# A Mixture-of-Experts stage: gate columns in one buffer, up columns in the other, and narrow down products in four column groups

## What is computed

```
def moe_swiglu(t, router, w_gate, w_up, w_down):
    logits = (t @ router).astype(jnp.float32)
    top_logits, top_idx = lax.top_k(logits, TOP_K)
    gates = jax.nn.softmax(top_logits, axis=-1)
    combine = jnp.sum(jax.nn.one_hot(top_idx, N_EXPERTS, dtype=jnp.float32) * gates[..., None], axis=1)
    out = jnp.zeros_like(t)
    for e in range(N_EXPERTS):
        out = out + combine[:, e:e + 1].astype(t.dtype) * swiglu(t, w_gate[e], w_up[e], w_down[e])
    return out
```

## Time and profile before

| | |
|---|---|
| three runs | 3126.87, 3130.53, 3133.26 us (median 3130.53) |
| span of the profiled execution | 3127.4 us |
| TensorE busy | 3027.5 us, 97% of the span |
| TensorE weight loads | 2197.5 us, 70% |
| VectorE, ScalarE busy | 1227.9 us, 482.9 us |
| read from HBM | 632.70 MB |
| chain that ended last | TensorE 84%, SyncE's queue 4%, VectorE 4%, DMA 3% |

### The profile page before, as it was taken

One profiled execution on the slowest core, in us unless ns is written; L12 is line 12 of the kernel. 1 busy time (PEld: TensorE's weight loads), 2 busy tenths in 40 slices (PEclk: granted clock), 3 DMA queues, 4 the chain that ended last, 5 costly groups with the idle time before them and its releaser, 6 DMA issues.

```text
span 3127.4 us, 44307 instructions
## 1 busy us (share of the span) xinstructions
PE 3027.5 (97%) x18487; PEld 2197.5 (70%) x18487; DVE 1227.9 (39%) x2576; ACT 482.9 (15%) x1092; POOL 109.9 (4%) x122
## 2 busy tenths in 40 slices
PE   7999998999999999999999999998999999999998
PEld 3566666588697677696786795876767677677765
DVE  2566666457466433366466365232001101101001
ACT  2332332010010023200212100221000000000001
POOL 1111112000000000000000000000000000000000
PEclk8999999999999999999999999998999999999999
DMA  7333116465355522364310465426999999999996
GB/s 252 119 109 128 54 55 260 158 221 164 125 187 166 160 68 74 94 203 162 103 58 14 123 202 162 126 64 214 379 381 377 355 382 375 341 380 380 337 379 253
DMA packets 418569, 636.83 MB, mean 204 GB/s; under 512 B 11950, under 2 KB 305429, under 8 KB 411069
## 3 DMA queue, kind: packets, MB, share of 16 engines
q1 hardware_dynamic: 413021, 612.49, 56.8%
q0 software_dynamic: 5344, 21.46, 2.0%
HBM read 632.70 MB, written 1.20 MB: 203 GB/s over the span
## 4 chain that ended last, share of the span: by engine, by line
PE 84%; SPq 4%; DVE 4%; DMA 3%; issue 1%; ACT 1%; DVEq 1%; PEld 1%; PEldq 0%; ACTq 0%
PE PS L1085 11%; PE PS L4106 11%; PE PS L1644 7%; PE PS L1105 7%; PE PS L4127 5%; PE PS L4113 5%; PE PS L1038 4%; PE PS L4153 3%; SPq L882 2%; PE PS L708 2%; PE PS L2220 2%; PE PS L3592 2%; PE PS L1119 2%; PE PS L2216 2%; PE PS L1794 1%
## 5 line engine op out<-in xcount | busy, mean ns | idle before, releaser
L1013 DVE TENSOR_TENSOR scratch<-scratch,PS 128x128 f32<-128x128 f32 x112 | 32.2, 288 | 618.2 <-ACT scratch L1003 618.2
L1644 PE MATMUL PS<-XT,WH 128*128 128x512 f32 x512 | 241.6, 597 | 1.7 <-ACT XT L485 1.7
L4106 PEld LDWEIGHTS PS<-scratch,WO 128*128 128x128 f32 x1792 | 208.6, 192 | 24.9 <-issue 24.3
L4106 PEld LDWEIGHTS PS<-scratch,WF 128*128 128x128 f32 x1792 | 202.2, 192 | 23.7 <-issue 20.3
L4106 PE MATMUL PS<-scratch,WO 128*128 128x128 f32 x1792 | 209.1, 275 | 0.0
L4106 PE MATMUL PS<-scratch,WF 128*128 128x128 f32 x1792 | 207.5, 277 | 1.5 <-DMA WF<-in_moe_wu 1.4
L1644 PEld LDWEIGHTS PS<-XT,WH 128*128 128x128 f32 x512 | 89.2, 192 | 69.1 <-issue 66.6
L1003 ACT ACTIVATE scratch<-PS 128x128 f32<-128x128 f32 x112 | 31.1, 278 | 616.8 <-PE PS L4106 616.8
L1085 PE MATMUL PS<-scratch 128*128 128x128 f32 x896 | 119.6, 277 | 0.0
L1085 PEld LDWEIGHTS PS<-scratch 128*128 128x128 f32 x896 | 110.4, 194 | 0.0
L4113 PE MATMUL PS<-WO,scratch 128*128 128x512 f32 x224 | 107.6, 603 | 0.0
(11 more groups left out here) (638 smaller groups left out, 5129.1 us busy)
## 6 DMA issues: line engine op xcount, KB each, us to landing
XT<-in_moe_wg SPq DMA_DIRECT2D x56, 1024.0 KB, 10.9
scratch<-in_moe_wu SPq DMA_DIRECT2D x56, 1024.0 KB, 14.1
OT<-in_moe_wd SPq DMA_DIRECT2D x56, 1024.0 KB, 14.1
WO<-in_ada_w SPq DMA_DIRECT2D x36, 1024.0 KB, 7.1
WF<-in_moe_wg SPq DMA_DIRECT2D x28, 1024.0 KB, 15.4
WF<-in_moe_wu SPq DMA_DIRECT2D x28, 1024.0 KB, 17.1
WF<-in_moe_wd SPq DMA_DIRECT2D x28, 1024.0 KB, 11.9
WO<-in_moe_wg SPq DMA_DIRECT2D x28, 1024.0 KB, 11.3
```

Of the source, the lines that this page charges most:

```text
L1644: mm = k.nc.tensor.matmul(k.PS[:, n % 2, :], k.gdn_w[n][:, kb, :], k.XT[:, kb, :], start=kb == 0, stop=kb == KB - 1)
L4106: mm = nc.tensor.matmul(k.PS[:, 4 + f, w * SLOTS:(w + 1) * SLOTS], slot.gu[:, w, kb, f * P:(f + 1) * P], k.xte[:, MANY, kb, :], start=kb = ...
```

## The change

Before and after, a fp32 product is two instructions of TensorE in the trace; the code and the lists of order below count products.

1. **Loads of the fuller expert.** Slot 0 now gets 512 columns of gate and slot 1 512 columns of up, as the emptier expert has it (`wide`); rows of 2 KB in place of 1 KB, and four issues of 1 MB as before. All four wait for `up1` of both slots, and both downs come behind them. The first block of ups waits for all four. The products themselves stay as they are, with the same sizes and in the same order. `up1` of slot 0 is still signalled after two blocks, that of slot 1 after the fourth.
2. **Downs of the emptier expert.** In place of 8 products of 64 columns x 512 there are 16 of 32 x 512, in four column groups: places 0 to 31 and 32 to 63, each for the left and the right half of the 1024 outputs. Both slots add into the same sums, which fill one bank (2) instead of two; `ye` gets 512 columns instead of 1024.
3. **Scatter of the emptier expert.** It now reads 64 rows per half: rows 0 to 63 of gates and sums for the left half, rows 64 to 127 for the right (`pair_sums`, `pair_scattered`).
4. **PSUM.** The emptier expert's gate and up now share bank 3; its ups no longer wait for the fuller one's products of VectorE. Silu (`few_silu_scalar`) now waits for `up1` of slot 1, which is the end of both, instead of slot 0.
5. **A third kind of step.** The functions with `tri` in their names are for pairs with a number of `FULL_PAIRS` or more. `FULL_PAIRS` is 4 and the pairs are 0 to 3, so none of these steps is run; the router's capacities come out as before, too, with one more VectorE instruction on the way to `ranked` and four small copies ahead of the logits.
6. `WF` and `WO` are now two parts of one tensor `W`.

```
...
+FULL_PAIRS = 4
...
@@ moe_sync
-                if kind == MANY:
-                    for s in range(2):
-                        cols = slice((2 * turn + s) * ROUND, (2 * turn + s + 1) * ROUND)
-                        gu = [w[:, ds(e, 1), :, cols].rearrange("p e kb n -> p (e kb) n") for w in ups]
-                        dn = downs[:, ds(e, 1), 4 * turn + 2 * s:4 * turn + 2 * s + 2, :]
-                        load_round(k, sp, slots[s], rnds[s], *gu, dn.rearrange("p e b n -> p (e b) n"))
-                    continue
                 for s in range(2):
                     for both in range(2):
                         sp.wait_ge(*slots[both].pe.at("up1", rnds[both] - 1))
...
@@ many_turn_tensor
-            if f == 0:
-                pe.wait_ge(slot.gu_in, (rnd + 1) * 32)
+            if (s, f) == (0, 0):
+                for both in range(2):
+                    pe.wait_ge(slots[both].gu_in, (rnds[both] + 1) * 32)
             for w in range(2):
                 for kb in range(KB):
-                    mm = nc.tensor.matmul(k.PS[:, 4 + f, w * SLOTS:(w + 1) * SLOTS], slot.gu[:, w, kb, f * P:(f + 1) * P],
+                    c = (2 * s + f) * P
+                    mm = nc.tensor.matmul(k.PS[:, 4 + f, w * SLOTS:(w + 1) * SLOTS], slots[w].wide[:, kb, c:c + P],
                                           k.xte[:, MANY, kb, :], start=kb == 0, stop=kb == KB - 1)
...
@@ few_down_tensor
+    pe.wait_ge(*k.few_act.at("flip", n))
     for s in range(2):
         pe.wait_ge(slots[s].dn_in, (rnds[s] + 1) * 16)
-    pe.wait_ge(*k.few_act.at("flip", n))
-    for f in range(2):
-        for half in range(2):
-            for s in range(2):
-                mm = k.nc.tensor.matmul(k.PS[ROWS[s], 2 + half, :], k.few_ht[:, f, s * FEW:(s + 1) * FEW],
+        for f in range(2):
+            for j in range(4):
+                half, c = j // 2, s * FEW + j % 2 * GROUP
+                mm = k.nc.tensor.matmul(k.PS[j * GROUP:(j + 1) * GROUP, 2, :], k.few_ht[:, f, c:c + GROUP],
                                         slots[s].dn[:, f, half * 512:(half + 1) * 512],
...
+def pair_sums(k, pair, kind, half):
+    if kind:
+        return ((k.gatedt[:, FEWER, :], slice(half * FEW, (half + 1) * FEW), k.ye[:, FEWER, 0:512]),)
+    if pair < FULL_PAIRS:
+        return ((k.gatedt[:, MANY, :], slice(0, P), k.ye[:, MANY, half * 512:(half + 1) * 512]),)
...
+def pair_scattered(k, pair, kinds, half, tile, bank, opens, closes):
+    parts = [part for kind in kinds for part in pair_sums(k, pair, kind, half)]
+    for n, (gates, rows, sums) in enumerate(parts):
+        mm = k.nc.tensor.matmul(k.PS[:, bank + half, :], gates[rows, tile * P:(tile + 1) * P], sums[rows, :],
+                                start=opens and n == 0, stop=closes and n == len(parts) - 1)
+    return mm
...
@@ few_silu_scalar
-    act.wait_ge(*slots[0].pe.at("up1", rnds[0]))
+    act.wait_ge(*slots[1].pe.at("up1", rnds[1]))
     for s in range(2):
-        act.activation(k.few_sg[ROWS[s], :], k.PS[ROWS[s], 4, 0:ROUND], ACT.Silu
+        act.activation(k.few_sg[ROWS[s], :], k.PS[ROWS[s], 3, 0:ROUND], ACT.Silu
...
@@ duo_sum_vector
-    k.nc.vector.tensor_copy(k.ye[:, kind, :], bank_rows(k, 2 * kind)).then_inc(*k.sums_dve.done(f"y{kind}"))
+    to, src = (k.ye[:, kind, 0:512], k.PS[:, 2, :]) if kind else (k.ye[:, kind, :], bank_rows(k, 0))
+    k.nc.vector.tensor_copy(to, src).then_inc(*k.sums_dve.done(f"y{kind}"))
```

More of the change, by code:

```diff
@@ L4019, in gather_products, with gates_turned @@
     return mm
-def gates_turned(k, u):
+def gates_turned(k, u, rest=False):
     for tile in range(2):
         mm = k.nc.tensor.transpose(k.PS[:, 6, tile * P:(tile + 1) * P], k.gated[:, u, tile, :], mat(k, C_ID))
+    for tile in range(2 if rest else 0):
+        mm = k.nc.tensor.transpose(k.PS[:, 6, L + tile * P:L + (tile + 1) * P], k.gated_rest[:, tile, :], mat(k, C_ID))
     return mm
@@ L4067, in duo_scatter_tensor @@
             pe.wait_ge(*k.duo_act.at("ga1", pair + 1))
-    scatter_products(k, kind, tile).then_inc(*k.sums_pe.done(f"sc{kind}{tile}"))
+    for half in range(2):
+        mm = pair_scattered(k, pair, (kind,), half, tile, 6, True, True)
+    mm.then_inc(*k.sums_pe.done(f"sc{kind}{tile}"))
 def gather_tensor(k, pe, e):
@@ L4214, in last_scatter_tensor @@
     for tile in range(2):
-        bank = (6, 4)[tile]
-        for kind in range(2):
-            if kind and not tile:
-                pe.wait_ge(*k.sums_dve.at("y1", pair))
+        if not tile:
             for half in range(2):
-                mm = k.nc.tensor.matmul(k.PS[:, bank + half, :], k.gatedt[:, kind, tile * P:(tile + 1) * P],
-                                        k.ye[:, kind, half * 512:(half + 1) * 512], start=kind == 0, stop=kind == 1)
+                pair_scattered(k, pair, (MANY,), half, 0, 6, True, False)
+            pe.wait_ge(*k.sums_dve.at("y1", pair))
+        for half in range(2):
+            mm = pair_scattered(k, pair, (MANY, FEWER) if tile else (FEWER,), half, tile, (6, 4)[tile], bool(tile), True)
         mm.then_inc(*k.sums_pe.both(*(("sc00", "sc01"), ("sc10", "sc11"))[tile]))
@@ L4352, in duo_choice_vector @@
     rank = pair + MANY_RANKS * kind
-    choice_vector(k, dve, kind, k.ranked[:, :, rank:rank + 1], k.few_iota if kind else k.slot_iota
-                  ).then_inc(*k.duo_dve.done(f"g{kind}"))
+    three = kind == MANY and pair >= FULL_PAIRS
+    i = choice_vector(k, dve, kind, k.ranked[:, :, rank:rank + 1], k.few_iota if kind else k.tri_iota if three else k.slot_iota)
+    if three:
+        for tile in range(2):
+            pos, gate = k.chosen_route[:, 0, tile:tile + 1], k.chosen_route[:, 1, tile:tile + 1]
+            k.nc.vector.tensor_scalar(k.gated_rest[:, tile, :], k.rest_iota, pos, gate, ALU.is_equal, ALU.mult)
+        i = dve.drain()
+    i.then_inc(*k.duo_dve.done(f"g{kind}"))
 def tokens_added(k, tile, bank=6):
@@ L4392, in duo_step_vector @@
     last = lambda f: slots[1].pe.at(f"down{f}", rnds[1] - 1)
-    for s in range(2):
+    if pair >= FULL_PAIRS:
+        for tile in range(2 if turn == 0 else 0):
+            duo_scatter_vector(k, dve, pair - 1, MANY, tile)
+        tri_vector(k, dve, n)
+    for s in range(2 if pair < FULL_PAIRS else 0):
         turn_vector(k, dve, slots, (s,), rnds, SLOTS, k.sgm, k.hidm, last, (0,))
```

161 lines of the change are left out of this document (139 added, 22 removed).

## The result

Of each kernel 7 runs stand against each other. The changed kernel takes 3144.12 us (median, 3138.52 to 3147.64), the kernel before 3131.20 (3125.04 to 3135.22): 1.0036 of it, with a 95% interval of 1.0025 to 1.0046. It is slower by 0.36%. The span of the profiled execution is 3136.4 us, 9.0 more than before.

The account below looks back on a forecast made before the run. TensorE was taken to bound the stage, DMA engines about 2% behind. Terms 4.7 + 2.0 - 1.8 + 2.1 + 0.5 - 4.8 - 0.5 = +2.2 us gave a 3129.6 span, 3133 us as median; range 3128 to 3139, 8 in 10 3125 to 3148.

Parts of the forecast that it names:

- Start of the stage: At the expert stage's start, the first up needs four loads instead of two and starts later: +4.7 us (3.6 to 5.5).
- Clock: First ups of the stage run at TensorE's lower clock after it stands idle about 6 us: +2.0 us (0 to 3.4).
- Pair 0: Rows of 2 KB speed the fuller expert's loads, so TensorE's weight waits in pair 0 go: -1.8 us (0 to -1.8).
- The loads of the ups wait longer: All four loads wait for the fourth block of ups; 21 steps miss by 0.1 us each: +2.1 us (0 to 16).
- the new ups miss every step: Rival: landing takes 15.0 us, so each of 21 steps waits 0.75 us: +16 instead of +2.1, 3147 us; chance 0.20.
- Scatter: Emptier expert's scatter, two 64-row products on different array halves; six on TensorE's path save 0.8 each: -4.8 us (-3.6 to -5.4).
- Last scatter: At the end, the narrower scatter saves for one tile only, the other alternating with full products: -0.5 us.
- Downs: Emptier expert's 32 down instructions of 32 columns run four at a time, 3.6 us as before: 0 (to +0.9 a step).
- Silu later: Silu begins after both gate and up, shrinking the transposition's cover from 0.67 to 0.25 us: +0.5 us over 28 steps.

Follow-up runs that it names:

- second profile: The changed kernel run once more with no edit and its own profile: 3142.05 us, 1.0031 of the kernel before.
- the run with 22 zero products: Changed kernel plus 22 products of a zero matrix behind the stage's first gather, into a bank nobody reads: 3140.43 us, 1.0028 of the kernel before.
- The version with the first step old: Changed kernel with gate slot released early and gate products before up products over two blocks, very first step loaded and multiplied as before: 3124.34 us, 0.9980.
- the two profiles of before: The kernel before, profiled originally and again in an unedited repeat; the repeat took 3133.43 us, 1.0003.
- old loads: Changed kernel with the fuller expert's loads, and the waits on them, as in the kernel before: 3127.16 us, 0.9983 of the kernel before.
- The early release: Changed kernel with the gate slot given back to SyncE after the gate products of the step's fourth block: 3132.12 us, 1.0007 of the kernel before.
- the split wait: Changed kernel whose first block's gate products wait for the gate slot alone, its up products for the up slot: 3127.91 us, 0.9989 of the kernel before.
- new loads alone: The kernel before with only the changed kernel's loads of the fuller expert and their waits: 3145.71 us, 1.0042.

## Why the prediction was right or wrong

The forecast was 3133 us, no change; the kernel takes 3144, slower by 0.36%, beyond the forecast's own 3128 to 3139 and inside the range of 8 in 10, near its upper end of 3148. By its own steps, from the first profile after:

- *Start of the stage:* +4.7 us forecast, 14.87 - 9.58 = +5.3 measured, within the bounds. The four megabytes landed 14.74 us after the first issue, not 14.3, and the first product starts 0.13 behind the landing.
- *Clock:* +2.0 forecast, 9.28 - 7.38 = +1.9 measured (9.55 in the second profile), and the run with 22 zero products showed its cause.
- *Pair 0:* -1.8 forecast. Its old waits are gone in every version with rows of 2 KB; the new ones stand in the next point. The version with the first step old shows it best: it starts like the kernel before (first up after 9.62 us) and has no waits in pair 0, where first up and waits there sum to 9.58 + 1.8 = 11.4 and 9.30 + 2.2 = 11.5 in the two profiles of before, and 10.95 + 0.3 = 11.2 with old loads. It differs from those in the order of products and release too, so the row size is borne out, not isolated.
- *The loads of the ups wait longer:* this is the step that failed, in its size. I wrote "I take a miss of 0.1 us in each step", 21 steps, +2.1 us. Measured are 5.9 us in 11 steps, and 8.7 in 14 in the second profile: where a step waits it waits 0.5 to 0.6 us on average, up to 1.19 and 1.50. The release came as forecast, at 18.17 to 18.21 us into a plain step against 18.15, and the landing too, at 14.3 in the middle of the 21 steps of the first profile (14.5 in the second). What the sum left out are the 0.14 us from the landing to the first product. They put the point that decides at 14.06, not at 14.26, so the landing of 14.3 that it took misses by 0.24, which in 21 steps is 5 us. The sum also had no term for the spread of the landings. The rival "the new ups miss every step" was said to decide from 14.5 on. It named the mechanism, but not every step misses. Its "against", that a step that waits lets the queue drain, is not shown: behind the waits of 0.4 us and more the next first megabyte landed anywhere from 5.2 to 7.0 us after its issue. The early release and the split wait each took all of it away, from either end.
- *Scatter:* -4.8 forecast. The row of the first narrow scatter saves 0.76, near the 0.8 of the forecast, but the product behind it gives 0.10 back (1.98 against 1.88 us), and the first step of a pair became shorter by 1.33 (42.86 to 41.53), twice 0.66: three pairs give -4.0. Of that, up to 1.8 us may have come back: the second steps of pairs 1 to 3, measured to the start of the third, take 33.37, 33.51 and 33.49 against 32.85, as the third begins with a wait. With new loads alone, where the first step is as long as before, they take 32.85, 33.16 and 32.85. A shorter first step leaves the queue less time to catch up, which would explain it; no run tests this by itself. These waits are part of the 5.9.
- *Last scatter:* -0.5 forecast. The 16 products take 7.26 us instead of 7.13, so +0.1. The weight loads show both sides of it:

```profile
3122.09 0.30 PEld L4062 LDWEIGHTS PS<-scratch 64*128 64x128 f32 x4 [0.76 <-issue]
3123.15 0.30 PEld L4062 LDWEIGHTS PS<-scratch 128*128 128x128 f32 x2 [0.76 <-issue]
3124.20 0.29 PEld L4062 LDWEIGHTS PS<-scratch 64*128 64x128 f32 x2 [0.76 <-issue]
```

The four narrow ones of the first tile take 3123.15 - 3122.09 = 1.06 us, where four full ones take 1.72. In the second tile two full ones, between narrow ones, take 3124.20 - 3123.15 = 1.05, where the kernel before had 0.43 for each. So the first tile gained about what was forecast, and the alternation in the second, counted as nothing, cost more than that.
- *Downs:* 0 forecast, 0 measured. The page of the Trainium skill, "TensorE: Matmul & The Clock Gate", Part 3, gives 2.38 times for three column tiles. The trace does not bear out the estimate of 4.5 us that the prediction worked out from it: 32 products of 32 columns take 3.64 us, where 16 of 64 columns took 3.65, with no loss by going from two groups to four.
- *Silu later:* +0.5 forecast, 0 measured, no idle time of TensorE at the transposition.

With the measured sizes: 5.3 + 1.9 - 1.8 + 5.9 - 4.0 = +7.3 us, and the stage is 973.94 - 966.36 = 7.6 us longer; the last scatter lies behind it. The second profile has 10.7 with 2.8 more of waits. Against this, the stretch behind the last scatter is 1.3 us shorter, though the last addition ends later: its last microseconds, behind the last store's landing, are 2.6 us before and 0.7 after. All versions with the new scatters have it, and its cause stays open. The medians differ by 12.9 and 9.8 us in the two comparisons, where the stages less that 1.3 give 6.3 and 9.3; what is between is not explained further. The first profile is of the fastest of its seven executions, 3138.52 against the median of 3144.12; the others may have waited more, as the second profile does, but that is not shown.

The chances: 0.20 stood on the missing ups, which would give 3147. What came is nearer to that rival than to the forecast. The sum was +2.2 us, and its terms came to +7.4 with the last scatter: the ups brought 3.8 more than forecast, the two scatter terms 1.4 and the start 0.6, and the silu 0.5 less. By these terms and the 1.3 behind the stage alone the time would be near 3137, inside the forecast's own range. The rest, up to 3144, no term foresaw, and that the range held it is owed to its upper end, which was set for the missing ups.

## What to carry to other kernels

When a buffer's release plus its landing comes within half a microsecond of the time it is needed, count the hand-over from landing to first product (0.14 us here) and count the term one-sidedly: early landings give nothing, late ones are paid in full. Time saved elsewhere can come back as such waits. Two buffers filled with wide rows need not be waited for together: if the products that read one come first and its release is signalled as soon as its last reader is through, the same loads cost nothing, here some 16 us against the version with a joint wait and release (0.9981 of the kernel before, against 1.0031 and 1.0036). Judge a mixed change by its parts: here the narrow scatters and column groups saved about 5 us while the loads lost 14.

## What was not expected of the hardware

The granted clock of an engine that had just been at 1.00 fell within a stand of 5.25 us even with 1.46 us of zero products ahead of it, and stayed at 1.00 over one of 0.52. Four loads of 1 MB in rows of 2 KB landed 14.4 to 14.8 us after their first issue at the stage's start, and 13.3 to 15.6 in the 21 steps of the changed kernel's two profiles, where four with a load in rows of 4 KB among them had taken 13.1 and 14.3. The slow ones mostly have one megabyte of 3.6 us or more instead of 2.7, or a first one that lands late. Four products of 64 rows in a row, on the array's two halves, take 1.06 us, where four of 128 rows take 1.82 or 1.72. Where two of them alternate with two of 128 rows, two of the full ones take 1.05 us instead of 0.86, and over the eight products of a tile this loses more than the four in a row gained (7.26 against 7.13 for all sixteen).
